# Fewer routing slots ahead of the first up projection, three tiles' choices in common steps, and idle products at the end

## The reference, cut to what matters

```python
g_logit = t @ wg + bg;  g_sel = argmax(g_logit)          # 4 groups
e_logit = (t @ we + be) of the chosen group              # 8 experts in a group
top_p, top_i = top_k(softmax(e_logit), 2)                # two experts for each token
y = sum over 32 experts of  c_e * ((silu(t @ w1_e) * (t @ w3_e)) @ w2_e)
```

## Time and profile before

| | us |
|---|---|
| median of 3 runs | 1040.34 |
| lowest and highest run | 1038.54, 1044.13 |
| the profiled execution, its own time | 1042.62 |
| span of its profile | 1040.9 |
| PE busy | 965.9 (93%) |
| DVE, ACT, POOL busy | 361.2, 248.6, 213.4 |
| chain that ended last: PE, DMA, DVE | 75%, 12%, 5% |
| memory read and written | 315.07 MB, 22.31 MB, 324 GB/s over the span |

### The profile page before, as it was taken

The page is one execution under the profiler, slowest core; times in us unless marked ns, Lnnn a source line. Parts: engine busy times, 40 slices in busy tenths (PEclk is TensorE's granted clock), DMA queues, the critical chain, the costliest instruction groups (busy, mean ns, idle before and its releaser), DMA issues.

```text
span 1040.9 us, 17790 instructions
## 1 busy us (share of the span) xinstructions
PE 965.9 (93%) x6151; PEld 612.3 (59%) x6152; DVE 361.2 (35%) x839; ACT 248.6 (24%) x538; POOL 213.4 (21%) x306
## 2 busy tenths in 40 slices
PE   5999999998998899998989899999998999998886
PEld 3444458555886555555555384878875555555552
DVE  4159494564346211110011271145434212221124
ACT  5110002445234122221221250033233111111112
POOL 1008300110001343332331100000002333332310
PEclk9999999999999899998998999999999999999999
DMA  9985545999715699999999899273647998999996
GB/s 357 312 267 172 194 133 214 320 343 380 313 40 208 240 393 406 406 405 407 407 406 407 322 310 328 82 265 108 222 157 242 399 400 301 407 405 404 403 405 248
DMA packets 129081, 315.90 MB, mean 303 GB/s; under 512 B 28891, under 2 KB 59891, under 8 KB 128996
## 3 DMA queue, kind: packets, MB, share of 16 engines
q1 hardware_dynamic: 113200, 295.93, 76.4%
q0 software_dynamic: 10800, 12.72, 3.6%
q10 hardware_dynamic: 4996, 6.09, 1.6%
HBM read 315.07 MB, written 22.31 MB: 324 GB/s over the span
## 4 chain that ended last, share of the span: by engine, by line
PE 75%; DMA 12%; DVE 5%; issue 3%; ACT 2%; SPq 1%; ACTq 0%; POOL 0%; POOLq 0%; DVEq 0%
PE ps L1137 18%; PE ps L941 16%; DMA ring<-in_moe_w 10%; PE ps L993 8%; PE ps L1163 8%; PE ps L951 5%; PE ps L895 3%; PE ps L1109 3%; PE ps L1147 1%; PE ps L1291 1%; SPq L709 1%; DMA pair_out<-RH,sidx_all 1%; DMA RAB<-pair_out 1%; PE ps L929 1%; PE ps L1236 1%
## 5 line engine op out<-in xcount | busy, mean ns | idle before, releaser
L1137 PE MATMUL ps<-ring,RT 128*64 128x256 f32 x2128 | 260.4, 398 | 27.0 <-DMA ring<-in_moe_w 24.2
L1137 PEld LDWEIGHTS ps<-ring,RT 128*64 128x64 f32 x2128 | 164.4, 143 | 97.7 <-issue 24.1
L941 PE MATMUL ps<-RT,ring 128*128 128x512 f32 (+1 forms) x544 | 182.0, 493 | 0.5 <-DVE RT L2309 0.5
L941 PEld LDWEIGHTS ps<-RT,ring 128*128 128x128 f32 x544 | 102.2, 190 | 76.5 <-issue 69.8
L2196 DVE TENSOR_TENSOR RT<-RT,ps 64x256 f32<-64x256 f32 x64 | 27.1, 423 | 270.1 <-ACT RT L1724 149.3
L1163 PE MATMUL ps<-ring,RT 128*64 128x512 f32 x424 | 100.4, 593 | 1.4 <-DVE RT L2202 1.0
L1724 ACT ACTIVATE RT<-ps 64x256 f32<-64x256 f32 x64 | 24.1, 377 | 257.5 <-PE ps L1137 236.3
L2351 DVE SCALAR_TENSOR_TENSOR RAB<-RM,chan,RAB 128x512 f32<-128x512 f32 x120 | 79.7, 748 | 0.0
L2600 POOL DMA_INDIRECT pair_out<-RH,sidx_all x62 | 63.1, 1018 | 55.5 <-POOL sidx_all L2597 51.0
L2576 POOL DMA_INDIRECT RH<-hrow,idx x7 | 8.1, 1156 | 307.5 <-DVE idx L2148 306.0
L2588 POOL DMA_INDIRECT RH<-hrow,sidx_all x56 | 59.2, 1057 | 49.4 <-issue 29.9
(11 more groups left out here) (282 smaller groups left out, 1000.6 us busy)
## 6 DMA issues: line engine op xcount, KB each, us to landing
ring<-in_moe_w SPq DMA_DIRECT2D x358, 512.0 KB
ring<-in_w_mod SPq DMA_DIRECT2D x96, 512.0 KB
ring<-in_odd_w_in SPq DMA_DIRECT2D x24, 512.0 KB
ring<-in_even_w_in SPq DMA_DIRECT2D x20, 512.0 KB
ring<-in_even_w_out SPq DMA_DIRECT2D x8, 512.0 KB
RAB<-in_moe_w SPq DMA_DIRECT2D x8, 512.0 KB, 7.8
RAB<-pair_out SPq DMA_DIRECT2D x8, 512.0 KB, 5.9
ring<-in_odd_w_out SPq DMA_DIRECT2D x8, 512.0 KB
```

Source lines behind the costliest of these rows:

```text
L941: mm = pe.matmul(bank, w[:, c, P * ft:P * (ft + 1)], moving[:, c, :], start=(c == 0), stop=(c == NCH - 1))
L1137: mm = pe.matmul(bank[CAP * k:CAP * (k + 1), 0:BLK], xt(c), w[k][:, BLK * c:BLK * (c + 1)], start=(c == 0), stop=(c == NCH - 1))
```

## The change

It has four parts.

1. `two_choices` for more than one tile (three tiles, in layer 0 alone): the per-tile steps become steps over all tiles; the fused comparison and multiply become separate instructions; instructions of different tiles run without a wait between them. For one tile nothing changes.
2. The slots get a third part. Part 1 is now the scatter rows of the first block and both rows of the second block. Part 2, the later blocks (six in layer 0, two in layer 1), has bank 6 in both layers. TensorE computes it behind U(0,0) instead of ahead of T(0,0); VectorE writes the comparisons hot(3) and later behind `extra_ready`, and converts part 2 in `last_slots`, behind hidden(0,0). `at_slot` has seven tiles instead of two, so that VectorE no longer waits for `slot_used`. TensorE waits for the drain of all banks behind T(0,1) as before, and this now takes in part 2. SP waits for part 2 ahead of `in_spare(5)`; GpSimd waits for `all_slots` ahead of an expert's second extra block.
3. In layer 0, five idle products are issued ahead of T(0,0), in bank 6. They wait for the drain of the bank's last user.
4. In the last group of four experts of each layer, two idle products in bank 7 are issued ahead of U of the third and the fourth expert.

```diff
@@ psum_plan, for each layer l
     add(("slots", 0, 1), "dve")
+    add(("slots", 0, 2), "dve", bank=SLOTS_BANK)        # SLOTS_BANK = 6
@@ tiles
-        at_slot = RM[:, 1136:1648].bitcast(F16).rearrange("p (b n s) -> p b n s", b=2, n=8)
+        at_slot = [where.bitcast(F16).rearrange("p (n s) -> p n s", n=8)
+                   for where in (RM[:, 1136:1392], RM[:, 1392:1648], RT[:, 1024:1280], RT[:, 1280:1536], RT[:, 2560:2816],
+                                 RT[:, 2816:3072], RT[:, 3072:3328])]
@@ SP, experts
                 sp.wait_ge(routed, l + 1)
                 if l == 1:
                     sp.wait_ge(first_full, 1)
+                full(sp, "slots", l, 2)
                 in_spare(5)
@@ TensorE, slot_rows
-                for b in range(n_blocks):
+                for b in range(2) if part == 1 else range(2, n_blocks):
                     pe.wait_ge(slot_hot, before + b + 2)
                     vs = slice(0, 2) if b else slice(1, 2)
-                    out = bank[:, EXPERTS * (2 * b - 1):EXPERTS * (2 * b + 1)] if b else bank[:, 0:EXPERTS]
-                    mm = rows(out, at_slot[:, (b + 1) % 2, :, :], vs)
-                    if b < n_blocks - 2:
-                        mm.then_inc(slot_used, 1)
+                    at_bank = (EXPERTS if b else 0) if part == 1 else 2 * EXPERTS * (b - 2)
+                    out = bank[:, at_bank:at_bank + (2 * EXPERTS if b else EXPERTS)]
+                    mm = rows(out, at_slot[(b + 1) % len(at_slot)], vs)
                 close(mm)
@@ TensorE, step
                     Hd(i, q - 1)
+                    if isinstance(i, int) and i == LAST_GROUP and q >= 2:
+
+                        pe.wait_ge(x_y_ready, pe.snap(extras))
+                        for _ in range(2):
+                            pe.matmul(ps[:, 7, 0:BLK], ident, const[:, 0:BLK], start=True, stop=True)
                     U(i, q)
@@ TensorE, start of the experts
                 if l == 0:
-                    emptied(0)
+                    emptied(0, 1)
                     T(0, 0, start=True)
-                emptied(2)
+                emptied(2, 1)
                 U(0, 0, start=(l == 0))
+                slot_rows(l, 2)
                 emptied(1)
                 T(0, 1, start=(l == 0))
@@ TensorE, layer 0
             slot_rows(0, 1)
+
+            warm(("slots", 0, 2), 5)
             experts(0)
@@ VectorE, two_choices
+                n = ts.stop - ts.start
+                if n > 1:
+                    place = const[:, C_PLACE:C_PLACE + EXPERTS].unsqueeze(1).broadcast_to([P, n, EXPERTS])
+                    for t in range(ts.start, ts.stop):
+                        step(dve.max(best[:, t, :], masked[:, t, :]), wait=False)
+                    step.sync()
+                    for out, k in ((in_two, 1), (cand, 0)):
+                        step(dve.tensor_tensor(out[:, ts, :], masked[:, ts, :], best[:, ts, k:k + 1].broadcast_to([P, n, EXPERTS]),
+                                               ALU.is_ge), wait=False)
+                    step.sync()
+                    step(dve.tensor_tensor(in_two[:, ts, :], in_two[:, ts, :], place, ALU.mult))
+                    step(dve.tensor_tensor(cand[:, ts, :], cand[:, ts, :], in_two[:, ts, :], ALU.add))
+                    for t in range(ts.start, ts.stop):
+                        step(dve.max(best_keys[:, t, :], cand[:, t, :]), wait=False)
+                    step.sync()
+                    step(dve.tensor_tensor(choices[:, :, ts, :], ...))
+                    return
@@ VectorE, route
-                for j in range(2, n_blocks + 1):
-                    hot(j)
+                hot(2)
...
-                step(dve.tensor_scalar(idx[:, 1:n_blocks, 0, :], later[:, :, 0, :], const[:, C_OFF:C_OFF + 1], None, ALU.add), wait=False)
                 step(dve.tensor_scalar(idx[:, 0, 1, :], bank[:, 0:EXPERTS], const[:, C_OFF + 1:C_OFF + 2], None, ALU.add), wait=False)
-                done(dve.tensor_scalar(idx[:, 1:n_blocks, 1, :], later[:, :, 1, :], const[:, C_OFF + 1:C_OFF + 2], None, ALU.add))
+                step(dve.tensor_scalar(idx[:, 1, 0, :], bank[:, EXPERTS:2 * EXPERTS], const[:, C_OFF:C_OFF + 1], None, ALU.add), wait=False)
+                done(dve.tensor_scalar(idx[:, 1, 1, :], bank[:, 2 * EXPERTS:3 * EXPERTS], const[:, C_OFF + 1:C_OFF + 2], None, ALU.add))
                 step.sync()
                 drained(dve, "slots", l, 1)
                 dve.tensor_copy(extra_i[0:1, l, :], words[0:1, :]).then_inc(extra_ready, 1)
+                for j in range(3, n_blocks + 1):
+                    hot(j)
@@ VectorE, experts
                 hidden(0, 0)
+                last_slots(l)
                 dve.wait_ge(extra_ready, l + 1)
@@ VectorE, new
+            def last_slots(l):
+
+
+                n = tiles_of[l] * P // CAP - 2
+                bank = full(dve, "slots", l, 2)
+                later = bank[:, 0:2 * EXPERTS * n].rearrange("p (b v e) -> p b v e", b=n, v=2)
+                step(dve.tensor_scalar(idx[:, 2:n + 2, 0, :], later[:, :, 0, :], const[:, C_OFF:C_OFF + 1], None, ALU.add), wait=False)
+                done(dve.tensor_scalar(idx[:, 2:n + 2, 1, :], later[:, :, 1, :], const[:, C_OFF + 1:C_OFF + 2], None, ALU.add))
+                step.sync()
+                drained(dve, "slots", l, 2)
+                dve.sem_inc(all_slots, 1)
@@ GpSimd, more
                         with pool.If(count > 1):
+                            pool.wait_ge(all_slots, l + 1)
                             with pool.Fori(0, count - 1) as k:
```

36 lines of the change are left out of this document (19 added, 17 removed).

## The result

The changed kernel takes 1043.85 us (median of 5 runs, 1041.19 to 1045.27) against 1039.32 (5 runs, 1038.54 to 1044.13) of the kernel before beside it: a ratio of 1.0039, with a 95% interval of 1.0023 to 1.0054. So it is slower by 0.35 to 0.4%, some 4 us, where 2.5 us faster was forecast, and the time lies outside the range. The profiled run took 1045.14 us, its span 1043.4, 2.5 more than the 1040.9 of before.

A forecast was written before the change was run, and what follows sets the result against it. DMA weight streaming was taken as the bound. Gains 1.8 + 0.9 + 1.7 = 4.4 from the profiled 1042.62 gave 1038.2; the routing gains alone, 2.7 from the median 1040.34, gave 1037.6; forecast 1037.8 us, range 1033.5 to 1041.5.

The forecast's parts named there:

- The bound and the pocket: Expert weight streams: DMA bounds them, an earlier start ends the layer earlier, later loads fit the idle pocket at no cost.
- Part 1: Layer 0 choices of three tiles in common steps: ranks start about 0.95 us earlier (bounds 0.5 and 1.15).
- Up to U(0,0), and its clock: Layer 0: U(0,0) starts at 339.4 rather than 342.19 and takes 3.67 us at the high clock, chance near 0.6.
- The terms behind U(0,0): Layer 0, up to Hd(0,0): later slots 2.2, conversions 0.8, count read 1.0, T(0,2) 0.65 us; Hd(0,0) 1.8 earlier.
- The count read: TensorE reading the extras' counts behind the bank 6 wait: exposed, 1.0 us (nothing if ahead, 1.5 at most).
- slots and drain: Layer 0 behind U(0,0): six later slot blocks, 2.2 us, then VectorE's conversions draining bank 6, 0.8 us.
- a hole over 2 us: Sign of a wrong prediction: TensorE idle over 2 us behind T(0,1), where about 1 us was expected.
- The mark: Start of Hd(0,0) in both layers, where gains were summed: 1.8 us earlier in layer 0, 0.9 in layer 1.
- Rival (a): First U stays slow: layer 0 loses 0.8 to 2, layer 1 0.8; 1042, up to 1043 us; chance 0.12.
- Idle products at the end: Before U(30) and U(31): free inside weight waits; layer 0's U(30) 1.7 us shorter, on the path; layer 1 nothing.
- The reference point: Profiled run 1042.62 is 2.3 us above the median 1040.34; slow U(30) and late products can be most of this.
- (c): Both first U, U(30) and late products at the high clock: 2.7 + 3.4 us gained, 1034.2; chance 0.20, elsewhere 0.22.

The follow-up runs named there:

- e16: The kernel before with seven idle products ahead of U(0,2) in layer 0: 1041.69 us, 1.0027 of the kernel before.
- e14: The changed kernel with nine idle products between the halves of tile 1's late products in layer 0: 1046.49 us, 1.0057 of the kernel before.
- e15: The kernel before with seven idle products ahead of U(0,1) in layer 0: 1041.52 us, 1.0034 of the kernel before.
- e1: The kernel before with only the new two_choices (three tiles in common steps): 1039.78 us, 0.9978 of the kernel before.
- e12: The changed kernel without the five idle products ahead of T(0,0) in layer 0: 1047.05 us, 1.0045 of the kernel before.
- e4: The changed kernel with the count read ahead of the later slots and the bank 6 wait moved to Dn(0,1): 1038.11 us, 0.9963 of the kernel before.
- e11: The same kernel as e4, measured and traced a second time: 1036.42 us, 0.9945 of the kernel before.
- e13: The kernel before, unchanged, measured once more for a second trace: 1039.20 us, 1.0008 of the kernel before.
- e8: The changed kernel with the next stage's weight loads held at layer 0's end until the pairs read back landed: 1043.65 us, 1.0041 of the kernel before.
- e7: The changed kernel without the idle products in the last group of each layer: 1045.81 us, 1.0056 of the kernel before.
- e2: The changed kernel with the old two_choices and without the idle products of the last group: 1049.16 us, 1.0084 of the kernel before.
- e5: The changed kernel, measured and traced a second time: 1043.15 us, 1.0034 of the kernel before.
- e10: The changed kernel with only the bank 6 wait moved to Dn(0,1), the count still read behind T(0,1): 0.9990 of the kernel before.
- e6: The changed kernel with only the count read moved ahead of the later slots, the bank 6 wait left: 1.0011 of the kernel before.

## Why the prediction was wrong

**The bound and the pocket: right.** The loop behind the start of a layer is fixed to 1 us in layer 0 (e16 apart) and to 1.5 in layer 1 (e14 apart), and the pocket without transfers is still there (share 0.01 from 357 to 363 us), so there is no sign that the transfers put later cost anything. e15 shows by a delay in layer 0 that a later start goes through to U(31).

**Part 1: right.** The last step of the three tiles ends at 326.34, 2.2 us after the first begins (2.3 forecast), and the ranks of layer 0 start at 330.04 where TensorE's timeline of before has 331.09. e1 has 0.22%, 2.3 us, against 0.95 foreseen; more than that I can't separate from the phase of its runs.

**Up to U(0,0), and its clock: right.** T(0,0) came at 337.68 (337.9 forecast), U(0,0) at 339.05 (339.4), 3.67 us long in both layers. For layer 0 the traces bear the idle products out: with them U(0,0) took 3.67 in all twelve traces, in the old order 5.3 to 6.5 in six and 3.67 in one (e16), and in e12, the new order without them, 6.03. For layer 1 the gain was booked against a slow U(0,0) that only two of the seven traces of the old order have.

**The terms behind U(0,0): one mis-sized.** The count read was put at 1.0, at most 1.5. It is 1.73 and 1.61. In layer 0 an error the other way (slots and drain took 2.4 us behind U(0,0) instead of 3.0) hid this, and Hd(0,0) came within 0.2 of the forecast. In layer 1 it was 1.1 late: 802.55 less the 1.65 by which the layer began late is 800.9, against 799.8. Of this 0.6 is the read, and 0.4 is T(0,2), which ran slowly behind the hole (1.03 us to Hd(0,0) where 0.6 was booked). I had even named a hole over 2 us as what would make the prediction wrong, and e4 and e11 show what it is worth.

**The mark: the step that failed.** The sum was made at Hd(0,0), as if what follows were unchanged. But I had read in the earlier trace rows that TensorE's clock falls where short products stand between holes, and then made a hole of 1.9 us myself and gave U(0,1) its 3.67. It took 5.13 and 4.60. At the end of U(0,1), layer 0 gains 0.5 us where 1.8 was booked, and layer 1 loses 1.2 where 0.9 was booked (after against before's profiled run; against e13 it loses 3.4). What the step is worth, e4 and e11 show: without the hole U(0,1) takes 3.67 in both layers, and the kernel is 0.7 to 0.9% faster than after. Rival (a) came nearest in time (1042, up to 1043), but by the wrong product: it is not the first U that is slow but the second. Its loss for layer 0 (0.8 to 2) didn't come, that for layer 1 (0.8) nearly did.

**Idle products at the end (part 4 of the change, headed part 3 in my text): the mechanism was right, the path wrong.** U(30) took 3.67, and the 1.7 us didn't arrive: U(31) began 0.41 earlier, all of which was there already at U(0,1)'s end. U(31) waits for weights, and those come a fixed time after the start of the layer. My sentence "it lies on the path" stood on the row of U(30), where the next one, U(31) of before, should have been read, which waits for the ring even behind the slow U(30):

```profile
577.33 3.67 PE L1137 MATMUL ps<-ring,RT 128*64 128x256 f32 x32 [0.92 <-DMA ring<-in_moe_w]
```

The Trainium skill ("TensorE: Matmul & The Clock Gate", section "What's actually happening") says that the activity check is free-running. The traces agree with what I drew from it: U(30) took 5.36 in the first trace of before and 3.67 in the second (e13), and the start of layer 1 differs by 2.2 us between the two.

**The end of layer 0: not foreseen, and only partly explained.** Both traces of after need 21.9 us from U(31) to the last late product, before 19.9 and 20.4; the others lie between 15.9 and 22.2, e1 lowest but one. These 2.0 us are most of the 2.5 between the two profiled runs. Shown is that the stand for the pairs differs (0 to 3.3 us), that it is there without the weight loads beside them (2.22 us in e8), and that the stretch is 2.3 us shorter when the late products behind the stand run at the full clock (21.9 in after, 19.6 in e14). Why the stand differs, and whether the change makes a longer one or the fall of the clock behind it likelier, stays open.

**The reference point.** I read before's profiled run (1042.62) as 2.3 us above the median and guessed the slow U(30) behind it. e13's profiled run (1041.26) lies 2.1 above its median too, with U(30) at 3.67, so the guess had no ground. Over the study profiled runs lie between 2.7 us below (e4) and 5.7 above (e7) their medians: the 2.3 says nothing. The slow U(0,0) of layer 1, which I took for the kernel's, was as much a matter of the run. A slip in the chances: (c) stands at 0.20 in one sentence and at 0.22 in another.

## What to carry to other kernels

When short work is moved from ahead of a large product to behind it, everything that the sequencer did in the shadow of that product (reading a count, a branch, a wait for a drain) comes into the open with it. Move the reads ahead of it and each wait to its first real user; here that turned a loss of 0.35 to 0.4% into a gain of 0.4 to 0.55%. Take the mark of a sum behind the first large product after the last hole you make, not ahead of it. And look at a second trace of the kernel before, before you book a slow product as something to be won.

## What the runs showed of the hardware

- A count read and the branch behind it cost 1.6 to 1.7 us in TensorE's queue when a wait stands ahead (after), though the load itself is 0.3 to 0.5 us, and nothing that shows when it is issued ahead of the slot products (e4, e11).
- Holes of 1.94 to 2.18 us between short products (T(0,1) and T(0,2)) were followed by a slow U(0,1) in 13 of 14 cases (both layers of after, e2, e5, e7, e8, e12 and e14), 4.60 to 6.17 us, the granted clock at 0.50 where it was read (after, e7), and not in all: after 2.18 us in layer 1 of e8 it took 3.67. The stands of 2.9 and 3.3 us in the late products of e4 and e11 left the clock up; 2.8 and 3.3 us in e5 and after brought it down.
- Ten idle rows take 2.4 us at a granted clock of 1.00 (after) and 4.6 at 0.50 (e10) at the same place, in kernels with the same TensorE instructions ahead. The end of U(0,1) then differs by 2 to 9 us; the runs of e6 alone ranged from 1035.4 to 1044.9.
